# Linear attention in a one-core decoder layer: heads alternated on the array, side work in other slots, two mean squares left in PSUM

## The chip, the cores and the metric

The kernel runs on one core of a Trainium2 chip. The metric is the device time of one launch in microseconds. The core has a matrix engine (TensorE, PE), a vector engine (VectorE, DVE), a scalar engine (ScalarE, ACT), GpSimd (POOL) and a queue for transfers (SyncE, SP). Each engine works through its own list of instructions in order; they meet through semaphores.

## The reference

One layer of a decoder over 512 tokens of width 1024, in float32:

```
h = x + 0.5 * rms(SwiGLU_1(rms(x)))       # D_FF 2816
h = h +       rms(Mixer(rms(h)))
h = h + 0.5 * rms(SwiGLU_2(rms(h)))

Mixer:  z = u @ w_in, split into
  FoX:  8 heads of 64, causal softmax of q.k/8 + sum of log f, 128-query blocks
  GLA:  4 heads, keys 64, values 128, chunks of 64 tokens:
        attn = tril(q_in k_in^T);  kv = k_st^T v per chunk
        S_c  = decay * S_(c-1) + kv_(c-1)
        o    = attn v + q_in S_c          # within the chunk + across chunks
        o    = rms(o) * gain * silu(g_r)
  y = sigmoid(gate_fox) * (o_fox @ w_f) + sigmoid(gate_gla) * (o_gla @ w_g);  y @ w_out
```

## The kernel before

Precision. The large products are float32 products in three float32r matmuls: every weight tile is split into `w_hi` (ScalarE, `split` at L693) and `w_lo` (VectorE, L1197) and every activation likewise, and hi*hi, hi*lo, lo*hi are added in PSUM (L1862 to L1864). The products inside the linear attention are plain float32 matmuls, each of which becomes two instructions. A split needs the raw tile from memory (SP's queue, four buffers) and frees the buffer once the remainder is taken.

The start. While the first tiles come in, TensorE runs `WARM` matmuls of a constant (`earliest_units`, L2052), which wait for VectorE's memset of that constant (L1528). The first real products (L2054) wait for splits of the first tiles.

The mixer's slots. After the first projections the attention runs in 38 slots `sl`, a loop that each engine has in its own version. There are 32 softmax steps (8 heads x 4 query blocks); step `sl` begins in slot `sl` and its probabilities are transposed in slot `sl + 2`. Beside them run filler products: 13 feature products (`FILLERS`; the last four are the output gates `gr`) in blocks of three matmuls of 512 columns, three blocks in slots with `sl % 4` of 0 or 1, two blocks at 2, none at 3. From slot 16 on, `FILLED` ends one in slots 18, 22, 26, 30, 34, and the tile of unit f + 4 is split behind it.

The order within a slot:
- TensorE: scores of step `sl` (L2136 to L2138), filler blocks, the linear attention's work of `gla_slots`, transposes of step `sl - 2` (L2209), and in slots 7, 11, 15, ... the product of probabilities and values (L2219).
- ScalarE: head and gate copies (`heads_and_gates`), copies of the chunk scores (`attn_copies`, L1028), exponential (L1061), rounding of the transposed probabilities (L1073), in slots 8, 12, ... half a head pair (L1081), in 13, 21, 29, 37 the pair's rounding (L1085), for an output its square and the rounding of that (L1097, L1101), for a mean square its copy (L1104), the scaled probabilities (L1107), a split.
- VectorE: maximum (L1682), head and gate remainders, reciprocal, the state recurrence (L1701, L1704), remainder of the probabilities (L1709), pair sums (L1715, L1720), the gate product (L1738), the normed output and the remainder of its square (L1743, L1745), the remainder of a split.

Linear attention. `gla_steps` lists 18 steps: two key transposes (`kst`), and for each pair of heads scores (`attn`), chunk states (`kv`), outputs (`o`), mean squares (`ms`). They take two banks in turn (`gbank`), so a step waits until the one two before has been read. Head 2j has its keys in partitions 0 to 63, head 2j + 1 in 64 to 127. Before, the matmuls of one head come after those of the other: scores of a head are four matmuls of 64 rows (L2171), an output is four of 128 rows within chunks (L2190) and seven of 64 rows across chunks (L2194). A mean square is one 128x128 average over the square's two parts (L2199, L2200), which waits for the remainder at L1745. In slot 36 ScalarE takes the logarithm of all four mean squares at once (L1116), then the exponential (L1118).

Of the kernel before, what the change touches and what calls it, by code (L numbers as in the profile page):

```python
# [23 lines left out]
P = 128  # L24
# [21 lines left out]
WARM = 9  # L46
# [80 lines left out]
PAIRS = 2  # L127


def macaron_layer(nc, h_store, x_t, g1cols, x, w1g, w1u, w1d, g1post, gmpre, w_in, b_forget, w_alpha, b_alpha,  # L130
                  gla_g, w_bf, w_bg, w_out, gmpost, g2pre, w2g, w2u, w2d, g2post, out):
    with ExitStack() as ctx:
# [207 lines left out]
        def gain(g):  # L340
# [22 lines left out]
        def fill_free(f):  # L363

            before = f - 2 if f < 9 else f - 1
            if before < 0:
                return (v_lo, TT) if f == 0 else (gv_out, TT)
            kind, n = FILLERS[before]
            return {"q": (q_lo, 2 * n + 2), "k": (k_lo, 2 * n + 2), "gq": (gq_out, n + 1), "gk": (gk_out, n + 1),
                    "gr": (gr_ready, n + 1)}[kind]  # L370

# [306 lines left out]
        def _(act):  # L678
# [370 lines left out]
            for sl in range(SLOTS_B):  # L1049
                if sl in FILLED and sl >= LATE:  # L1050
                    heads_and_gates(FILLED[sl])
                for g in gla_slots.get(sl, ()):
                    if gla_steps[g][0] == "attn":
                        attn_copies(gla_steps[g][1], g)
# [31 lines left out]
                if sl == 9:  # L1086
                    act.wait_ge(a_dve, 5)
                    nc.scalar.activation(ga, gb, ACT.Exp, scale=-1.0 / TAU).then_inc(a_act, 1)
                for g in gla_slots.get(sl, ()):
# [5 lines left out]
                    if kind == "o":  # L1095
                        act.wait_ge(o_ready, n + 1)
                        nc.scalar.activation(msq[:, n, :], gbank(g), ACT.Square).then_inc(sq_ready, 1)  # L1097
                        act.wait_ge(sq_ready, n + 1)
                        if n:
                            act.wait_ge(gms_ready, n)  # L1100
                        nc.scalar.activation(sq_hi, msq[:, n, :], ACT.Copy).then_inc(sq_hi_out, 1)  # L1101
                    if kind == "ms":
                        act.wait_ge(gms_ready, n + 1)
                        nc.scalar.activation(msq[:, n, :], gbank(g), ACT.Copy).then_inc(ms_out, 1)  # L1104
# [4 lines left out]
                if sl in FILLED:  # L1109
                    v = U_FILL + FILLED[sl]  # L1110
                    split(v + 4)
# [79 lines left out]
        def _(dve):  # L1191
# [484 lines left out]
            for sl in range(SLOTS_B):  # L1676
# [7 lines left out]
                if sl in FILLED and sl >= LATE:  # L1684
                    heads_and_gates(FILLED[sl])
                if sl < NS:
# [23 lines left out]
                if sl >= 8 and sl % TT == 0:  # L1710
                    hh = sl // TT - 2
                    dve.wait_ge(half_out, hh + 1)
                    if hh >= 2:
                        dve.wait_ge(fox_hi, hh // 2)
                    V.tensor_tensor(pair_sum[FOX_D * (hh % 2):FOX_D * (hh % 2) + FOX_D, :], bank[0:FOX_D, B_OT, :], half_sum,  # L1715
                                    ALU.add).then_inc(pair_ready, 1)
                if sl >= 13 and (sl - 13) % 8 == 0:
                    p = (sl - 13) // 8
# [14 lines left out]
                if sl in gated_slots:  # L1733
                    n = gated_slots[sl]
                    dve.wait_ge(gr_ready, n + 1)
                    dve.wait_ge(on_ready, n + 1)
                    tile = arena[:, T_OG[n], :]
# [685 lines left out]
```

## Time and profile before

| | us |
|---|---|
| median of 3 runs | 1055.09 |
| lowest and highest | 1054.83, 1055.9 |
| the profiled execution's own time | 1056.04 |
| its span, first to last instruction | 1054.3 |

| engine | busy us | share of the span |
|---|---|---|
| TensorE | 1046.2 | 99% |
| VectorE | 816.1 | 77% |
| ScalarE | 568.0 | 54% |
| GpSimd | 44.7 | 4% |

Busy time is the union of an engine's instructions. Matmuls overlap in the array, so the difference of two starts, not a duration, is what one costs in a stream. The slots in question lie between about 459 and 540 us.

### The profile page before, as it was taken

What the parts mean: (1) busy time and instruction counts of PE and PEld (TensorE: products, weight loads), DVE (VectorE), ACT (ScalarE), POOL (GpSimd) and SP (SyncE); (2) the same over time, 40 slices, a digit from 0 to 9 for tenths busy, and PEclk for the clock granted to TensorE, in tenths of its full rate; (3) what the DMA queues carried; (4) which work ended last, traced back from release to release, by engine and by line L of the source; (5) the groups of instructions that cost most, each with busy time, mean ns of one, the idle gap of its engine ahead of it and who ended that gap; (6) DMA issues with size and microseconds to landing.
All of it is one profiled execution on the core that took longest, in us unless ns stands there. A gap on an engine that the chain in (4) does not pass through costs nothing.

```text
span 1054.3 us, 16505 instructions
## 1 busy us (share of the span) xinstructions
PE 1046.2 (99%) x6657; PEld 947.8 (90%) x6657; DVE 816.1 (77%) x971; ACT 568.0 (54%) x816; POOL 44.7 (4%) x98
## 2 busy tenths in 40 slices
PE   9999999999999999999999999999999999999997
PEld 7899999998888988888888999889899999998886
DVE  6998989989985583467689775558778878789964
ACT  6555455456654683567776344344454544566542
POOL 2000000000001310001000000021000000000001
PEclk9999999999999999999999999999999999999999
DMA  9623422451152553232120347315524224450052
GB/s 298 201 80 94 147 81 81 153 202 46 33 191 59 182 151 105 66 89 73 41 81 20 102 133 229 118 42 179 160 80 155 86 81 133 147 200 1 1 200 80
DMA packets 111835, 121.28 MB, mean 115 GB/s; under 512 B 6512, under 2 KB 92544, under 8 KB 111760
## 3 DMA queue, kind: packets, MB, share of 16 engines
q1 hardware_dynamic: 108544, 115.47, 34.3%
q10 hardware_dynamic: 2240, 2.11, 0.9%
q0 software_dynamic: 976, 2.66, 0.7%
q8 instruction: 53, 0.87, 0.3%
q14 instruction: 22, 0.18, 0.1%
HBM read 111.80 MB, written 6.29 MB: 112 GB/s over the span
## 4 chain that ended last, share of the span: by engine, by line
PE 91%; DVE 3%; ACT 2%; issue 1%; SPq 1%; DMA 1%; POOL 0%; ACTq 0%; DVEq 0%; POOLq 0%
PE bank L1961 13%; PE bank L1962 13%; PE bank L1960 13%; PE bank L1872 8%; PE bank L1862 5%; PE bank L2022 5%; PE bank L2023 5%; PE bank L2024 5%; PE bank L1864 5%; PE bank L1863 5%; PE bank L1927 1%; PE bank L1929 1%; PE bank L1928 1%; PE bank L2113 1%; PE bank L2112 1%
## 5 line engine op out<-in xcount | busy, mean ns | idle before, releaser
L1961 PE MATMUL bank<-tc,w_hi 128*128 128x256 f32 x576 | 163.3, 283 | 0.0
L1962 PE MATMUL bank<-tc,w_lo 128*128 128x256 f32 x576 | 163.3, 283 | 0.0
L1960 PE MATMUL bank<-tc,w_hi 128*128 128x256 f32 x576 | 163.2, 283 | 0.0
L1962 PE MATMUL bank<-u_hi,w_lo 128*128 128x256 f32 x504 | 142.9, 283 | 0.0
L1961 PE MATMUL bank<-u_lo,w_hi 128*128 128x256 f32 x504 | 142.8, 283 | 0.0
L1960 PE MATMUL bank<-u_hi,w_hi 128*128 128x256 f32 x504 | 142.8, 283 | 0.0
L1303 DVE TENSOR_TENSOR w_lo<-h,w_hi 128x1024 fp32r<-128x1024 f32 x72 | 87.8, 1222 | 33.6 <-ACT w_hi L765 33.6
L1962 PEld LDWEIGHTS bank<-tc,w_lo 128*128 128x128 f32 x576 | 110.8, 192 | 0.0
L1960 PEld LDWEIGHTS bank<-tc,w_hi 128*128 128x128 f32 x576 | 110.8, 192 | 0.0
L1961 PEld LDWEIGHTS bank<-tc,w_hi 128*128 128x128 f32 x576 | 110.8, 192 | 0.0
L1197 DVE TENSOR_TENSOR w_lo<-raw,w_hi 128x1024 fp32r<-128x1024 f32 x57 | 69.5, 1221 | 42.3 <-ACT w_hi L693 42.1
L765 ACT ACTIVATE w_hi<-h 128x1024 fp32r<-128x1024 f32 x72 | 75.8, 1053 | 41.1 <-PE bank L1962 26.0
L1960 PEld LDWEIGHTS bank<-u_hi,w_hi 128*128 128x128 f32 x504 | 96.9, 192 | 0.2
L1961 PEld LDWEIGHTS bank<-u_lo,w_hi 128*128 128x128 f32 x504 | 96.9, 192 | 0.2
L1962 PEld LDWEIGHTS bank<-u_hi,w_lo 128*128 128x128 f32 x504 | 96.9, 192 | 0.0
L2022 PE MATMUL bank<-w_hi,a_hi 128*128 128x512 f32 x224 | 87.3, 390 | 0.0
L2023 PE MATMUL bank<-w_lo,a_hi 128*128 128x512 f32 x224 | 87.3, 390 | 0.0
L2024 PE MATMUL bank<-w_hi,a_lo 128*128 128x512 f32 x224 | 87.3, 390 | 0.0
L1303 DVE TENSOR_TENSOR w_lo<-raw,w_hi 128x1024 fp32r<-128x1024 f32 x54 | 66.0, 1223 | 24.1 <-ACT w_hi L765 24.1
L693 ACT ACTIVATE w_hi<-raw 128x1024 fp32r<-128x1024 f32 x57 | 60.1, 1056 | 44.1 <-PE bank L1872 16.7
L809 ACT ACTIVATE scr<-bank 128x512 f32<-128x512 f32 x63 | 37.6, 598 | 81.8 <-PE bank L1962 81.8
L1862 PE MATMUL bank<-u_hi,w_hi 128*128 128x512 f32 x200 | 80.3, 401 | 0.1
(313 smaller groups left out, 2511.1 us busy)
## 6 DMA issues: line engine op xcount, KB each, us to landing
raw<-in_w_in SPq DMA_DIRECT2D x28, 512.0 KB, 3.9
raw<-in_ffn_w_down SPq DMA_DIRECT2D x20, 512.0 KB, 6.5
h<-in_ffn_w_gate SPq DMA_DIRECT2D x9, 1024.0 KB, 5.5
h<-in_ffn_w_up SPq DMA_DIRECT2D x9, 1024.0 KB, 8.7
raw<-in_ffn_w_gate SPq DMA_DIRECT2D x9, 1024.0 KB, 5.4
raw<-in_ffn_w_up SPq DMA_DIRECT2D x9, 1024.0 KB, 8.1
h<-in_w_in SPq DMA_DIRECT2D x6, 1024.0 KB, 7.0
h<-in_ffn_w_down SPq DMA_DIRECT2D x8, 512.0 KB, 6.6
```

The lines of the kernel that those rows point to most:

```text
L693: nc.scalar.activation(w_hi[:, slot(u), :], raw[:, slot(u), :], ACT.Copy).then_inc(hi_ready, 1)
L765: nc.scalar.activation(w_slot(w_hi, u), w_source(layer, q, n), ACT.Copy).then_inc(hi_ready, 1)
L1197: V.tensor_tensor(w_lo[:, slot(u), :], raw[:, slot(u), :], w_hi[:, slot(u), :].bitcast(F32), ALU.subtract).then_inc(lo_ready, 1)
L1303: V.tensor_tensor(w_slot(w_lo, u), w_source(layer, q, n), w_slot(w_hi, u).bitcast(F32), ALU.subtract).then_inc(lo_ready, 1)
L1862: mm(dst, w_hi[:, slot(u), w], rhs_hi[:, k - k0, :], start=k == k0, stop=False)
L1872: last = mm(bank[:, 2 * t + c, :], a[:, s, toks], w[:, s, c * HALF:(c + 1) * HALF], start=first and a is a_hi and w is w_hi, stop=final an ...
L1960: mm(dst, w_hi[:, slot(u), w], moving(n, 0, k, sums), start=first and k == 0, stop=False, skip_group_check=True)
L1961: mm(dst, w_hi[:, slot(u), w], moving(n, 1, k, sums), start=False, stop=False, skip_group_check=True)
L1962: last = mm(dst, w_lo[:, slot(u), w], moving(n, 0, k, sums), start=False, stop=k == KD // 2 - 1, skip_group_check=True)
L2022: mm(dst, a_hi[:, s, toks], w_hi[:, s, cols], start=start, stop=False, skip_group_check=True)
L2023: mm(dst, a_hi[:, s, toks], w_lo[:, s, cols], start=False, stop=False, skip_group_check=True)
L2024: last = mm(dst, a_lo[:, s, toks], w_hi[:, s, cols], start=False, stop=False, skip_group_check=True)
```

## The change

Five things change together.
- `gla_steps` runs each kind for both heads of a pair before the next kind, and the matmuls of the two heads are alternated one by one (`chunk_scores`, `chunk_states`, `chunk_outputs`). Their waits are joined: states wait for all four score copies, outputs for all four masks and the whole recurrence.
- New slots: `gla_slots`; squares and remainders by `norm_slots`, score copies by `copy_slots`, mean copies by `mean_slots`, gate products by `gated_slots` (and ahead of the reciprocal), the pair remainder by `fox_rest_slots`, splits 7 to 11 by `hi_slots` and `lo_slots`.
- The mean squares of heads 2 and 3 are not copied out; the logarithm reads their banks, so it becomes two instructions.
- The warming matmuls become 32 of 128 columns, from 9 of 512.
- VectorE writes their constant first.

```diff
-WARM = 9
+WARM = 32
...
-            gla_steps += [("attn", 2 * j), ("attn", 2 * j + 1), ("kv", 2 * j), ("kv", 2 * j + 1),
-                          ("o", 2 * j), ("ms", 2 * j), ("o", 2 * j + 1), ("ms", 2 * j + 1)]
+            gla_steps += [(kind, 2 * j + e) for kind in ("attn", "kv", "o", "ms") for e in range(2)]
...
-        gla_slots = {13: (0,), 15: (1,), 17: (2, 3), 18: (4, 5), 20: (6,), 22: (7, 8), 24: (9, 10), 25: (11, 12),
-                     26: (13,), 28: (14,), 30: (15, 16), 32: (17,)}
-        gated_slots = {25: 0, 29: 1, 33: 2, 37: 3}
+        gla_slots = {13: (0,), 15: (1,), 17: (2, 3), 18: (4, 5), 20: (6, 7), 21: (8,), 22: (9,),
+                     24: (10, 11), 25: (12, 13), 28: (14, 15), 29: (16,), 30: (17,)}
+        norm_slots = {20: 0, 21: 1, 28: 2, 29: 3}
+        copy_slots = {17: (0, 1), 25: (2, 3)}
+        mean_slots = {22: 0, 23: 1}
+        gated_slots = {23: 0, 27: 1, 31: 2, 35: 3}
+        fox_rest_slots = {13: 0, 23: 1, 31: 2, 37: 3}
+        hi_slots = {19: 7, 23: 8, 24: 9, 27: 10, 31: 11}
+        lo_slots = {22: 7, 24: 8, 25: 9, 30: 10, 33: 11}
...
                 if sl == NS + 4:
-                    act.wait_ge(ms_out, GLA_H)
-                    nc.scalar.activation(msq, msq, ACT.Ln, scale=4.0, bias=eps_t[:, :]).then_inc(gla_act, 1)
-                    act.wait_ge(gla_act, 1)
+                    act.wait_ge(ms_out, 2)
+                    act.wait_ge(gms_ready, GLA_H)
+                    nc.scalar.activation(msq[:, 2:4, :], bank[:, B_GLA[0]:B_GLA[0] + 2, :], ACT.Ln, scale=4.0,
+                                         bias=eps_t[:, :]).then_inc(gla_act, 1)
+                    nc.scalar.activation(msq[:, 0:2, :], msq[:, 0:2, :], ACT.Ln, scale=4.0, bias=eps_t[:, :]).then_inc(gla_act, 1)
+                    act.wait_ge(gla_act, 2)
...
+            V.memset(mean_g[:, :].bitcast(F32), 1.0 / GLA_DV).then_inc(hidden_ready, PAIRS)
             V.memset(eps_t[:, :], 4 * EPS).then_inc(merged, TILES)
             V.memset(bias_small[:, :], 0.0).then_inc(bias_set, 1)
             V.memset(c_neg[:, :].bitcast(F32), 0.0)
-            V.memset(mean_g[:, :].bitcast(F32), 1.0 / GLA_DV).then_inc(hidden_ready, PAIRS)
...
                 for _ in range(WARM):
-                    mm(bank[:, 7, :], mean_g[:, :], c_neg[:, :], start=True, stop=True)
+                    mm(bank[:, 7, 0:P], mean_g[:, :], mean_g[:, :], start=True, stop=True)
...
+            def chunk_scores(j, *banks):
+
+                if j == 0:
+                    pe.wait_ge(kst_copied, 2)
+                    pe.wait_ge(a_dve, 7)
+                    pe.wait_ge(k_lo, 2 * FOX_H // 2)
+                else:
+                    pe.wait_ge(ms_out, 2)
+                for t in range(TT):
+                    toks = slice(t * P, (t + 1) * P)
+                    for e in range(2):
+                        rows = slice(64 * e, 64 * e + 64)
+                        last = mm(banks[e][:, toks], arena[rows, T_GK + j, toks], arena[rows, T_GQ + j, toks],
+                                  start=True, stop=True)
+                        if t == TT - 1:
+                            last.then_inc(attn_ready, 1)
+
+            def chunk_states(j, *banks):
+
+                pe.wait_ge(kst_copied, 2)
+                pe.wait_ge(attn_copied, 4 * j + 4)
+                for c in range(NCH - 1):
+                    odd = c % 2
...
+            def chunk_outputs(j, *banks):
+
+                pe.wait_ge(attn_masked, 4 * j + 4)
+                pe.wait_ge(state_ready, (NCH - 1) * (j + 1))
+                for e in range(2):
+                    n = 2 * j + e
+                    for t in range(TT):
+                        mm(banks[e][:, t * P:(t + 1) * P], arena[:, T_GV + t, n * GLA_DV:(n + 1) * GLA_DV],
+                           intra[:, e, t, :], start=t == 0, stop=False, skip_group_check=True)
+                for c in range(1, NCH):
+                    cols = slice(c * CHUNK, (c + 1) * CHUNK)
+                    for e in range(2):
+                        rows = slice(64 * e, 64 * e + 64)
+                        last = mm(banks[e][:, cols], state[rows, c, :], arena[rows, T_GQ + j, cols],
+                                  start=False, stop=c == NCH - 1, skip_group_check=True)
...
             pe.wait_ge(on_ready, GLA_H)
-            pe.wait_ge(ms_out, GLA_H)
...
                 if f == 1:
                     pe.wait_ge(fox_lo, FOX_H // 2)
+                    pe.wait_ge(gla_act, 1)
```

## Rows read from the trace of the kernel before

**Rows 1.** Busy time, share of the span and instructions, from the page.

```profile
PE 1046.2 (99%) x6657; PEld 947.8 (90%) x6657; DVE 816.1 (77%) x971; ACT 568.0 (54%) x816; POOL 44.7 (4%) x98
```

**Rows 2.** Stage table: length, busy by engine (instructions), clock, DMA share, GB/s.

```profile
485.00:511.00 26.00, 25.41 (x165) 21.46 (x165) 16.90 (x39) 18.85 (x43) 1.49 (x4) 1.00 0.20 51
```

**Rows 3.** Order of time, TensorE's 64-row bursts: start, us, engine, line, operands, count.

```profile
476.94 1.71 PE L2171 MATMUL bank<-arena 64*128 64x128 f32 x16
...
481.02 1.37 PE L2181 MATMUL bank<-arena,scr 64*64 64x128 f32 x28
...
488.98 1.77 PE L2194 MATMUL bank<-arena,scr 64*128 64x64 f32 x14
...
504.10 1.16 PE L2171 MATMUL bank<-arena 64*128 64x128 f32 x8
...
509.31 1.09 PE L2181 MATMUL bank<-arena,scr 64*64 64x128 f32 x16
...
512.76 0.87 PE L2181 MATMUL bank<-arena,scr 64*64 64x128 f32 x12
```

**Rows 4.** Waits between 440 and 575 us: who for whom, total, times, longest.

```profile
PEld bank L2190 <- DVE scr L1704: 0.9, 1, 0.9
...
PEld bank L2171 <- ACT scr L1104: 0.5, 1, 0.5
```

**Rows 5.** Order of time after the third output's burst, slots 28 and 29.

```profile
520.85 0.55 PE L2209 MATMUL bank<-ident,scr 128*128 128x128 f32 x3
...
523.65 0.60 PE L2209 MATMUL bank<-ident,scr 128*128 128x128 f32 x4
...
523.96 0.68 DVE L1745 TENSOR_TENSOR a_lo<-scr,a_hi 128x512 fp32r<-128x512 f32 x1
...
525.96 0.63 ACT L1085 ACTIVATE a_hi<-scr 128x512 fp32r<-128x512 f32 x1
```

**Rows 6.** Order of time, TensorE in slot 22: scores, then behind two filler blocks.

```profile
493.84 0.42 PE L2136 MATMUL bank<-qk 128*128 128x384 f32 x1
...
495.79 0.39 PE L2199 MATMUL bank<-a_hi,mean_g 128*128 128x512 f32 x1
```

**Rows 7.** Order of time, ScalarE and VectorE, slots 25 and 26.

```profile
509.42 0.78 ACT L1028 ACTIVATE scr<-bank 64x256 f32<-64x256 f32 x2 [0.96 <-PE bank L2171]
...
514.55 2.27 DVE L1704 SCALAR_TENSOR_TENSOR scr<-scr,decay,bank 128x128 f32<-128x128 f32 x6
...
514.87 1.04 ACT L693 ACTIVATE w_hi<-raw 128x1024 fp32r<-128x1024 f32 x1
```

**Rows 8.** Order of time, the first 12 us.

```profile
0.86 0.06 DVE L1525 MEMSET eps_t<- 128x1 f32 x1 [0.86 <-PEq L2407]
...
1.49 0.17 DVE L1528 MEMSET mean_g<- 128x128 f32 x1
...
1.71 4.21 PE L2052 MATMUL bank<-c_neg,mean_g 128*128 128x512 f32 x9 [1.71 <-DVE mean_g L1528]
...
5.72 0.63 PE L2054 MATMUL bank<-u_hi,w_hi 128*128 128x512 f32 x1
5.72 0.33 PEld L2054 LDWEIGHTS bank<-u_hi,w_lo 128*128 128x128 f32 x1
...
7.00 0.42 PE L2054 MATMUL bank<-u_hi,w_lo 128*128 128x512 f32 x1
...
7.72 0.19 PEld L2054 LDWEIGHTS bank<-u_hi,w_lo 128*128 128x128 f32 x1
...
10.95 0.69 DVE L1543 TENSOR_TENSOR w_lo<-raw,w_hi 128x512 fp32r<-128x512 f32 x1 [0.57 <-ACT w_hi L899]
```

**Rows 9.** Order of time, two matmuls of 128 columns at the high clock, slot 16.

```profile
471.60 0.28 PE L2136 MATMUL bank<-qk 128*128 128x128 f32 x1
...
471.71 0.27 PE L2137 MATMUL bank<-qk,a_hi 128*128 128x128 f32 x1
```

**Rows 10.** Transfers, from the page: queue, count, KB each, us to landing.

```profile
raw<-in_w_in SPq DMA_DIRECT2D x28, 512.0 KB, 3.9
```

More of the change, by code:

```diff
@@ L1051, in _ @@
                     heads_and_gates(FILLED[sl])
[L1052 to L1054 removed]
+                for n in copy_slots.get(sl, ()):
+                    attn_copies(n, gla_steps.index(("attn", n)))
+                if sl in mean_slots:
+                    n = mean_slots[sl]
+                    act.wait_ge(gms_ready, n + 1)
+                    nc.scalar.activation(msq[:, n, :], gbank(gla_steps.index(("ms", n))), ACT.Copy).then_inc(ms_out, 1)
                 if sl < NS:
@@ L1108, in _ @@
                                          scale=rinv[:, sl:sl + 1]).then_inc(probs_ready, 1)
-                if sl in FILLED:
-                    v = U_FILL + FILLED[sl]
-                    split(v + 4)
+                if sl in FILLED and FILLED[sl] not in hi_slots.values():
+                    split(U_FILL + FILLED[sl] + 4)
+                if sl in hi_slots:
+                    split(U_FILL + hi_slots[sl] + 4)
                 if sl - 1 in FILLED and FILLERS[FILLED[sl - 1]][0] == "k":
@@ L1732, in _ @@
                     V.tensor_tensor(kin, kin, ga, ALU.mult).then_inc(a_dve, 1)
[L1733 to L1737, printed above, removed]
-                    V.tensor_tensor(tile, tile, arena[:, T_GR[n], :], ALU.mult).then_inc(og_raw, 1)
-                for g in gla_slots.get(sl, ()):
-                    kind, n = gla_steps[g]
-                    if kind == "o":
-                        dve.wait_ge(sq_ready, n + 1)
-                        V.tensor_scalar(arena[:, T_OG[n], :], gbank(g), gn[:, n:n + 1], None, ALU.mult).then_inc(on_ready, 1)
-                        dve.wait_ge(sq_hi_out, n + 1)
-                        V.tensor_tensor(sq_lo, msq[:, n, :], sq_hi.bitcast(F32), ALU.subtract).then_inc(sq_lo_out, 1)
-                if sl - 1 in FILLED:
+                if sl in norm_slots:
+                    n = norm_slots[sl]
+                    dve.wait_ge(sq_ready, n + 1)
+                    V.tensor_scalar(arena[:, T_OG[n], :], o_bank(n), gn[:, n:n + 1], None, ALU.mult).then_inc(on_ready, 1)
+                    dve.wait_ge(sq_hi_out, n + 1)
+                    V.tensor_tensor(sq_lo, msq[:, n, :], sq_hi.bitcast(F32), ALU.subtract).then_inc(sq_lo_out, 1)
+                if sl - 1 in FILLED and FILLED[sl - 1] not in lo_slots.values():
                     split(U_FILL + FILLED[sl - 1] + 4)
+                if sl in lo_slots:
+                    split(U_FILL + lo_slots[sl] + 4)
             def gate_t_lo(n):
@@ L2118, in _, with key_transposes @@
             pe.wait_ge(v_lo, TT)
-            read = {"kst": lambda n: (kst_copied, n + 1), "attn": lambda n: (attn_copied, 2 * n + 2),
-                    "kv": lambda n: (state_ready, (NCH - 1) * (n // 2 + 1)), "o": lambda n: (on_ready, n + 1),
-                    "ms": lambda n: (ms_out, n + 1)}
+            def key_transposes(g, n):
+                dst = gbank(g)
+                if n == 0:
+                    pe.wait_ge(gv_out, TT)
+                    pe.wait_ge(a_dve, 6)
+                else:
+                    pe.wait_ge(kst_copied, 1)
+                for t in (2 * n, 2 * n + 1):
+                    for j in range(2):
+                        c = (t % 2) * 2 * P + j * P
+                        last = nc.tensor.transpose(dst[:, c:c + P], arena[:, T_KST + j, t * P:(t + 1) * P], ident[:, :])
+                last.then_inc(kst_ready, 1)
@@ new lines, in chunk_states @@
+            def chunk_states(j, *banks):
[3 more added lines that the diff above has]
+                    odd = c % 2
+                    rows = slice(CHUNK * odd, CHUNK * odd + CHUNK)
+                    for e in range(2):
+                        hh = 2 * j + e
+                        last = mm(banks[odd][64 * e:64 * e + 64, (c // 2) * P:(c // 2 + 1) * P],
+                                  kst_tok[rows, c // 2, hh * GLA_DK:(hh + 1) * GLA_DK],
+                                  arena[rows, T_GV + c // 2, hh * GLA_DV:(hh + 1) * GLA_DV], start=True, stop=True)
+                    if c >= NCH - 3:
+                        last.then_inc(kv_ready, 1)
@@ L2185, in _ @@
-                    if kind == "o":
-                        pe.wait_ge(attn_masked, 2 * n + 2)
-                        pe.wait_ge(state_ready, (NCH - 1) * (n // 2 + 1))
-                        rows_k = slice(64 * (n % 2), 64 * (n % 2) + 64)
-                        for t in range(TT):
-                            mm(dst[:, t * P:(t + 1) * P], arena[:, T_GV + t, n * GLA_DV:(n + 1) * GLA_DV],
-                               intra[:, n % 2, t, :], start=t == 0, stop=False, skip_group_check=True)
-                        for c in range(1, NCH):
-                            cols = slice(c * CHUNK, (c + 1) * CHUNK)
-                            last = mm(dst[:, cols], state[rows_k, c, :], arena[rows_k, T_GQ + n // 2, cols],
-                                      start=False, stop=c == NCH - 1, skip_group_check=True)
-                        last.then_inc(o_ready, 1)
```

83 lines of the change are left out of this document (31 added, 52 removed).

## The prediction

> **What bounds the kernel now.** I read the page's busy times first: TensorE is busy 1046.2 of 1054.3 us [rows 1], so the time is the length of TensorE's own stream plus its few waits. The table by stage says whether another engine stands close behind where the change is made: from 485 to 511 us TensorE is busy 25.41 of 26.00, ScalarE 18.85, VectorE 16.90 [rows 2]. ScalarE and VectorE work there in turns (a maximum on VectorE, an exponential on ScalarE, a copy, a remainder on VectorE), so 18.85 and 16.90 of 26 leave little air once both must follow in turn. Then I went along TensorE in order of time for the linear attention's bursts [rows 3], to the waits for the one real stall [rows 4], and along all three engines through the slot that follows an output burst [rows 5]. Last, the first 12 us, because the warming matmuls change [rows 8].
>
> **Part 1, alternating heads.** The busy times of the bursts [rows 3]: scores 1.71 us for heads 0 and 1 together and 1.16 each for 2 and 3 (two such rows); states 1.37 for the first pair, 1.09 and 0.87 for the second; the inter-chunk half of an output 1.77, four times. A burst of 64-row matmuls for one head uses half the array. That two halves run side by side is seen in the first scores row: 16 instructions take 1.71 where 8 take 1.16, so part of head 1 already ran beside head 0. The first states row says the same (28 in 1.37, against 16 in 1.09). I take it that alternated bursts last as long as the longer head alone: scores 2 x 1.16, states 2 x 1.09, inter-chunk outputs 2 x 1.77. Saved: 4.03 - 2.32 = 1.71, 3.33 - 2.18 = 1.15, 7.08 - 3.54 = 3.54, together 6.4 us of TensorE. The intra-chunk matmuls use all rows and stay. Bounds: 0 if alternation buys nothing; 6.4 is the most. I take 6.4, since the overlap is in rows of the same lines.
>
> Two old waits may go. At the first output TensorE starts 0.90 after its last start, 0.67 beyond the usual 0.23, and its weights wait 0.9 for the recurrence; at head 3's scores it is 0.23 beyond, and the weights wait 0.5 for a mean copy [rows 4]. Moving splits 7 and 8 out of ScalarE's slots 15 and 18 (1.04 each) and their remainders out of VectorE's slots 16 and 19 lets the state recurrence (0.29 for the first copy, then 2.27 for six steps [rows 7]) end before TensorE asks, so I count both as gone: 0.9. Credit of the stage: 7.3 us.
>
> **Part 2, the new slots: what is late next.** Within a slot TensorE does scores, filler products, linear attention, and only then the transposes of the step two back. ScalarE does exponential, rounding of the transposed probabilities, head copies, and only then the square of the output and its rounding; VectorE's remainder ends the chain and the mean-square matmul waits for it.
> - Mean square 0 goes from slot 22 to 21, and 2 likewise into 29, one slot after the burst. The chain from the end of the burst is in the trace: burst over at 520.85, then ScalarE's copies, square and rounding, and VectorE's remainder ends at 523.96 + 0.68 = 524.64, 3.8 us later. TensorE has three transposes, scores and nine filler matmuls to do meanwhile: 520.85 to 523.65, 2.8 us [rows 5]. It waits 1.0 us, twice: 2.0.
> - Mean squares 1 and 3 come in slots 22 and 30. Their chain starts with the four transposes after the mean square before: 0.6 until they are ready, copy 0.5, the pair's rounding 0.63 [rows 5], square 0.63, rounding and remainder 0.76 + 0.68: 3.9. TensorE has those transposes (0.36) and scores with six filler matmuls (493.84 to 495.79, 1.95 [rows 6]): 2.3. It waits 1.6, twice: 3.2.
> - The states of heads 2 and 3 (slot 25) now wait for all four score copies. From the end of the first output burst (0), with the durations above and the starts 0.1 closer than durations as neighbours on an engine are: mean square 0 at 3.85, mean square 1 at 8.2. ScalarE: gate tanh and mean copy (0.6 each), exponential 22 at 8.9. VectorE: gate product (0.7), remainder of split 7 (1.22) to 11.1, maximum 23 to 11.8. ScalarE: exponential 23 at 11.8, copy, probabilities at 12.8, split 8 (1.04) at 13.45, exponential 24 at 14.4, copies at 15.1 and 15.6, probabilities, split 9 at 16.35, then four score copies (0.78 for two [rows 7]) 17.3 to 18.9. TensorE: slot 23 from 8.65, slot 24 from 10.7, scores burst 13.4 to 14.5, slot 25 from 14.8, at the states at 17.3. It waits 1.6.
> - VectorE then does the recurrence (2.6), a remainder, split 9's remainder (1.22) and the maximum. The transposes of slot 27 wait 0.3 for it, the scores of slot 28 0.8 for the exponential behind it: 1.1. Behind them in TensorE's queue stands the second output burst.
> - The last product of probabilities and values already waits for VectorE; 0.1 more.
> New waits: 2.0 + 3.2 + 1.6 + 1.1 + 0.1 = 8.0. Bounds: 0 if the chains shorten, 11 if the slot-25 wait doubles and each slot slips as much again. Stage: 8.0 - 7.3 = +0.7 us.
>
> **Part 3, mean squares left in their banks.** Two copies of about 0.6 (its other 512-column copies) leave ScalarE; the logarithm becomes two of half size, the same work. It stands behind the last values product, beside 48 filler-like gate matmuls (11 us) in which no TensorE wait shows: 0. If that cover were gone it would cost one more fixed part of an instruction, about 0.1. The new wait of gate unit 1 for the first logarithm is met long before. SP's queue: the later remainders of splits 7 to 11 free their raw buffers later, and the loads behind them start up to six slots (20 us) later. The first is gate unit 2's, freed in slot 22 and split in slot 31; such loads land in 3.9 us [rows 10]: 0. The masks on GpSimd follow the score copies and are done slots before the outputs: 0.
>
> **Part 4, the start.** The warming matmuls go from 9 of 512 columns to 32 of 128, and the constant is written first on VectorE: 0.86 in place of 1.49, so warming starts at 1.1 in place of 1.71. Today nine last to about 5.55 (the first real one starts at 5.72), 0.43 apart, and TensorE's clock rises from 1.2 to 2.4 GHz at about 7.0, where the durations drop from 0.63 to 0.42 [rows 8]. What a 128-column matmul with a weight load costs at the high clock is in the trace: starts 0.11 apart [rows 9], though its columns alone would need 0.06; the weight load sets the pace. At the low clock no row shows the pair. Below: 0.107, a quarter of 0.43. Above: 0.22, twice 0.11. The load's own duration grows from 0.19 to 0.33 [rows 8], by 0.14; a load of one column per clock would grow by 0.05, one that takes 0.11 at the high clock by 0.11. So I take 0.22, less a little. Then 27 to 29 are done when the clock rises at 7.0 and the rest take 0.11: real work starts at about 7.5 at the high clock. Before, 6 of its matmuls had gone by then: 6 x 0.23 = 1.3 us late, and TensorE never idles afterwards to give it back. The most an early start could bring is 0.1: the weights of the third stretch are ready at 10.95 + 0.69 = 11.64 [rows 8], where TensorE arrives at 11.83. Bounds: -0.1 and +2.5 (all 32 at the low clock end at 8.2, and the clock stays low for the first 1.3 us of the real work, as today: by 9.5 three products are done, where 14 were). Taken: +1.3.
>
> The Trainium skill (TensorE: Matmul & The Clock Gate, section LDWEIGHTS) gives a weight load as its columns over 1.2 GHz, whatever the contraction size. For 128 columns that is 107 ns; the trace agrees at the high clock, 0.11. If the rule held unchanged at the low clock, 32 would take 3.4 us, the start would wait for data instead, and its term would be -0.1, as in rival B below; the grown duration speaks against it.
>
> **The sum.** +0.7 + 1.3 = +2.0 on the profiled execution's own 1056.04 (span 1054.30 and 1.74 around it): 1058.0. That execution is 0.95 above the median of the runs shown, 1055.09, so on that scale 1057.1.
>
> **Rivals.**
> - A, faster: the saving arrives. The waits at the mean squares (5.2) stay, but ScalarE and VectorE, relieved early, keep up in slots 24 to 28, so the 2.7 of slots 25 to 28 vanish. Stage -2.1; with a start at -0.1 1052.9, with all waits but one chain gone as low as 1048. For it: both have over 7 us idle in 26 [rows 2]. Against: they work in turns, and two splits land where TensorE no longer gives them 2.7 us of output burst per head as cover. It decides when the copies of slot 25 are done before 17.3 us after the first burst.
> - B, the start costs nothing (load at the low clock 0.107, or the clock rises earlier): stage +0.7, 1055.7. For: a weight load could keep a pace of its own, and no row shows one that sets the pace at the low clock. Against: its duration grew by 0.14.
> - C, the clock rises later: start +2.5, 1058.3. For: no row fixes the moment of the rise to the start of work. Against: TensorE would be at work from 1.1 us without a break, earlier than now.
> - D, the alternation does not overlap: 6.4 comes back less the waits it would have filled (about 4): 1059.5. Against: the first scores row.
>
> **Chances.** Forecast (both waits and a late start) 0.38, A 0.24, B 0.20, C 0.12, D 0.06. A measurement of this kernel tells about 0.2% (2.1 us) from no change, so the lines are 1053.0 and 1057.2. The forecast lies on the upper one: half of it and most of C and D are slower (0.36); B and the other half same (0.38); A and the lucky side of B faster (0.26). Range 1050.8 to 1059.6; it leaves out the deepest form of A and the worst of C and D.
>
> **What would show it.** TensorE's inter-chunk row should read 28 instructions in about 1.8 us, twice. The first real matmul should start at about 7.5, not 5.7; if it starts at 4.9, the start step is wrong. Idle time before the mean-square matmuls should be 1.0, 1.6, 1.0, 1.6; if it is under 1 in all, the chain step is wrong and A holds. The states of slot 25 should wait for ScalarE's score copies. From the last values product on, every gap should be as before.

## The result: 0.6% slower, outside the forecast

The changed kernel takes 1061.1 us (median of 6 runs, 1060.4 to 1061.91), the kernel before 1055.18 beside it on the same chip (6 runs, 1054.56 to 1055.9): ratio 1.0056, 95% interval 1.0043 to 1.0069. Forecast was 1057.1, with 1059.6 as the upper end. The sum had the direction right (slower), though it gave a slower kernel a chance of 0.36 only; the size was wrong.

Three moments of the profiled execution divide its 5.7 us of longer span (1054.3 before, 1060.0 after): the first scores matmul of slot 0, the last values product, and the end. Starts in the kernel before: 412.34 and 538.23; after:

```profile
415.76 0.22 PE L2212 MATMUL bank<-qk 128*128 128x128 f32 x1
...
543.56 1.51 PE L2251 MATMUL bank<-pt,og 128*128 128x512 f32 x8
```

So everything up to slot 0 lost 3.42 us, slots 0 to 34 (called the stage below) went from 125.89 to 127.80 us (+1.91), and the rest from 516.1 to 516.4 (+0.4). The forecast had +1.3, +0.7 and 0.

The page's busy line, and the stage table over 26 and 27 us that answers to [rows 2] (start:end, length, then busy time and instructions of PE, PEld, DVE, ACT, POOL, then the granted clock, DMA share, GB/s):

```profile
PE 1046.1 (99%) x6680; PEld 947.8 (89%) x6680; DVE 816.5 (77%) x971; ACT 567.1 (54%) x815; POOL 44.6 (4%) x98
...
485.00:511.00 26.00, 23.36 (x159) 19.20 (x159) 18.11 (x42) 18.85 (x43) 0.00 (x0) 1.00 0.11 31
511.00:538.00 27.00, 22.76 (x163) 19.35 (x163) 17.95 (x38) 16.55 (x39) 1.64 (x4) 0.94 0.15 40
```

TensorE's total is what it was: up to slot 0 it is busy 4.1 us longer, because it starts 0.6 earlier and the longer start counts as work, and in slots 0 to 34 it is busy 4.4 less (120.90 against 125.26). In the stage it now idles 2.6 of 26 and 4.2 of 27 us, where 0.6 of 26 and none of 27 was idle before; neither ScalarE nor VectorE is full. They take turns.

The start, in order of time (start, duration, engine, line); it answers to [rows 8]:

```profile
0.89 0.17 DVE L1538 MEMSET mean_g<- 128x128 f32 x1 [0.89 <-PEq L2439]
...
1.11 7.09 PE L2067 MATMUL bank<-mean_g 128*128 128x128 f32 x32 [1.11 <-DVE mean_g L1538]
8.00 0.73 PE L2069 MATMUL bank<-u_hi,w_hi 128*128 128x512 f32 x1
8.53 0.63 PE L2069 MATMUL bank<-u_hi,w_lo 128*128 128x512 f32 x1
...
12.36 0.63 PE L2069 MATMUL bank<-u_lo,w_hi 128*128 128x512 f32 x2
12.82 0.40 PE L2069 MATMUL bank<-u_hi,w_hi 128*128 128x512 f32 x1
```

All 32 warming matmuls stand 0.21 us apart (the last ends at 8.2), and matmuls of 512 columns keep 0.43 between starts until about 12.3; before, that ended at 7.0. From then on they stand 0.23 apart. The clock column reads 1.00 through this stretch in both kernels, so here only the spacing shows the clock: 0.43 is also what the same matmuls keep at 516.31, 516.74 and 517.16 us, where the column does read 0.50. Below, "the pace breaks" means the moment at which 0.43 becomes 0.23.

The stage in order of time on TensorE, idle time before a row in brackets; it answers to [rows 3, 5]:

```profile
480.32 1.16 PE L2161 MATMUL bank<-arena 64*128 64x128 f32 x16
483.84 1.09 PE L2175 MATMUL bank<-arena,scr 64*64 64x128 f32 x28
...
489.98 2.02 PE L2188 MATMUL bank<-scr,arena 128*128 128x128 f32 x16 [0.37 <-DVE scr L1723]
491.93 1.78 PE L2194 MATMUL bank<-arena,scr 64*128 64x64 f32 x28
497.58 0.48 PE L2229 MATMUL bank<-a_hi,mean_g 128*128 128x512 f32 x1 [0.95 <-DVE a_lo L1758]
501.90 0.47 PE L2229 MATMUL bank<-a_hi,mean_g 128*128 128x512 f32 x1 [1.32 <-DVE a_lo L1758]
...
507.08 1.16 PE L2161 MATMUL bank<-arena 64*128 64x128 f32 x16
513.09 1.09 PE L2175 MATMUL bank<-arena,scr 64*64 64x128 f32 x28 [1.93 <-ACT scr L1036]
...
524.44 1.78 PE L2194 MATMUL bank<-arena,scr 64*128 64x64 f32 x28
530.09 0.47 PE L2229 MATMUL bank<-a_hi,mean_g 128*128 128x512 f32 x1 [0.99 <-DVE a_lo L1758]
534.41 0.47 PE L2229 MATMUL bank<-a_hi,mean_g 128*128 128x512 f32 x1 [1.33 <-DVE a_lo L1758]
```

Against [rows 3]: 28 matmuls of both heads last 1.78, where 14 of one head lasted 1.77. The brackets are the waits: the first (0.37) was 0.51 before, the others are new. One thing in no forecast stands behind the longest of them, in the clock column (third figure from the right; same columns as above):

```profile
512.00:514.00 2.00, 0.91 (x28) 0.88 (x28) 0.44 (x2) 1.47 (x5) 1.59 (x4) 1.00 0.33 73
514.00:516.00 2.00, 2.00 (x12) 1.89 (x9) 1.64 (x5) 0.73 (x2) 0.05 (x1) 0.52 0.63 189
516.00:518.00 2.00, 2.00 (x6) 1.54 (x7) 1.93 (x5) 0.26 (x1) 0.00 (x0) 0.62 0.00 0
```

The granted clock fell to its lower level, 1.2 GHz, from 514.1 to 517.5; the wait of 1.93 us had ended 1.0 before. It may not do so in every launch. Outside the profiled execution only the mean clock of a launch hints at it, and weakly (beside the first batch of experiments the kernel before has 0.997 or 0.998 in eight of 31 launches too): of the six launches of the changed kernel three have 0.997 or 0.998 (1061.35 to 1061.91 us, the profiled one among them) and three have 1.00 (1060.40 to 1060.85).

### The profile page after: what moved, and what is told of

It is laid out like the page before. It is cut to its first block, busy times and chain, and to the rows that moved or that the text cites. A ratio compares the mean times of both kernels' runs of the same rounds, so it can differ in the third digit from the quotient of the medians.

```text
span 1060.0 us, 16547 instructions
## 1 busy us (share of the span) xinstructions
PE 1046.1 (99%) x6680; PEld 947.8 (89%) x6680; DVE 816.5 (77%) x971; ACT 567.1 (54%) x815; POOL 44.6 (4%) x98
## 4 chain that ended last, share of the span: by engine, by line
PE 95%; DVE 2%; ACT 1%; issue 1%; POOL 0%; DVEq 0%; POOLq 0%; ACTq 0%
PE bank L1977 13%; PE bank L1976 13%; PE bank L1975 13%; PE bank L1887 9%; PE bank L1877 5%; PE bank L1879 5%; PE bank L1878 5%; PE bank L2037 5%; PE bank L2039 5%; PE bank L2038 5%; PE bank L2069 2%; PE bank L1942 1%; PE bank L1944 1%; PE bank L1943 1%; PE bank L2127 1%; PE bank L2129 1%
```

## Experiments

Twelve kernels in three batches; the kernel before ran beside each (medians 1055.63, 1055.48 and 1055.83). The ratios are to it. "Old start" is nine warming matmuls of 512 columns and the old order of the constants.

### The start and the stage, one at a time

**a_oldstart**: the change with the old start.

```
-WARM = 32
+WARM = 9
-            V.memset(mean_g[:, :].bitcast(F32), 1.0 / GLA_DV).then_inc(hidden_ready, PAIRS)   # first
+            ... (behind c_neg, as before)
-        mm(bank[:, 7, 0:P], mean_g[:, :], mean_g[:, :], start=True, stop=True)
+        mm(bank[:, 7, :], mean_g[:, :], c_neg[:, :], start=True, stop=True)
```

> The changed kernel with the start of before (9 warming matmuls of 512 columns, the constant written fourth). Theory S (the start costs what the two traces show, 3.4 us, and nothing downstream gives it back): 1061.1 - 3.4 = 1057.7 us, clock at 2.4 GHz from about 7.0 us. Theory M (only the mixer's slots made it slower, the start's delay was partly covered later): within 1 us of 1061.1. If the fall of the clock near 514 us hangs on where the kernel stands in time, it may go away too, and the time is 1056.5 or less.

Measured 1057.57 us, ratio 1.0016 (1.0006 to 1.0025): theory S. The clock still falls in the stage.

**b_newstart**: the kernel before with the new start alone.

> The kernel of before with only the new start (32 warming matmuls of 128 columns, the constant first). Theory S: 1055.2 + 3.4 = 1058.6 us, the clock at 2.4 GHz only near 12.3 us and the first real product at about 8.0. Theory M: within 1 us of 1055.2.

Measured 1058.44 us, ratio 1.0025 (1.0015 to 1.0034): theory S. Its trace repeats the start of the change: warming 7.09 us long, first real matmul at 8.00, and a break of pace at about 12.3:

```profile
1.11 7.09 PE L2052 MATMUL bank<-mean_g 128*128 128x128 f32 x32 [1.11 <-DVE mean_g L1525]
...
12.29 0.63 PE L2054 MATMUL bank<-u_lo,w_hi 128*128 128x512 f32 x2
12.76 0.39 PE L2054 MATMUL bank<-u_hi,w_hi 128*128 128x512 f32 x1
```

The start costs 2.8 us by the medians of b_newstart, 3.5 by those of the change and a_oldstart, which did not run side by side; the stage costs 1.9 (a_oldstart). Each alone is slower than before, so both halves of the change lose.

**b_17x128**: the kernel before with 17 warming matmuls of 128 columns, which take as long as its nine of 512 (`WARM = 17`, and the operand `mean_g` over 128 columns); the constants stay in the old order.

> The kernel of before with 17 warming matmuls of 128 columns in place of 9 of 512, the constant where it was: at 0.213 each they end at about 5.5, as the nine do, so the first real product starts when it did. It separates two parts of the start's loss. Theory L (short matmuls paced by their weight loads do not bring the clock up): the clock rises well after 7.0, near 10 to 12 us, and each microsecond of that costs half: 1056.5 to 1057.5 us. Theory T (32 were simply too long): the clock rises at 7.0 and the time is 1055.2 within 0.4.

Measured 1056.47 us, ratio 1.0006 (0.9997 to 1.0016): the time alone does not decide. The trace does:

```profile
1.71 3.89 PE L2052 MATMUL bank<-mean_g 128*128 128x128 f32 x17 [1.71 <-DVE mean_g L1528]
5.40 0.73 PE L2054 MATMUL bank<-u_hi,w_hi 128*128 128x512 f32 x1
...
9.77 0.86 PE L2054 MATMUL bank<-u_lo,w_hi 128*128 128x512 f32 x2
10.47 0.40 PE L2054 MATMUL bank<-u_hi,w_hi 128*128 128x512 f32 x1
```

The real work starts as early as ever (5.40) but runs at the low pace until about 10.5. In the eight profiled executions with the old start, the pace broke between 4.9 and 7.8. So the length of the warming alone does not explain the loss: its form counts. The late break costs less here because the real work started on time; slot 0 begins at 413.40, where it is 411.3 to 412.3 with the old start and 415.6 to 415.8 with the new one.

**b_early512**: the kernel before, the constant first, ten warming matmuls of 512 columns that read the constant's 128 columns four times.

```
+                mm(bank[:, 7, :].rearrange("p (a c) -> p a c", a=4), mean_g[:, :],
+                   mean_g[:, :].rearrange("p (o c) -> p o c", o=1).to_broadcast([P, 4, P]), start=True, stop=True)
```

> The kernel of before with the constant first and 10 warming matmuls of 512 columns (the constant read four times over), from 1.1 to about 5.55 us. If the earlier start of work brings the clock up earlier, up to 0.2 us are gained (1055.0) before the third stretch of products waits for its weights; if the clock rises at 7.0 all the same, no change.

Measured 1055.18 us, ratio 0.9994 (0.9985 to 1.0004). A gain over the kernel before is not shown. But work goes on from 1.1 us, as in the change, and on the same constant, only in long matmuls, and the pace is up with the first real one. So neither the early start of work nor the constant that is read delayed the pace in the change:

```profile
1.11 4.61 PE L2052 MATMUL bank<-mean_g 128*128 128x512 f32 x10 [1.11 <-DVE mean_g L1525]
5.54 0.41 PE L2055 MATMUL bank<-u_hi,w_hi 128*128 128x512 f32 x1
```

### Is the saving of the alternation real?

**s_headbyhead**: old start, the slots of the change, the pairs head by head.

```
-                for c in range(NCH - 1):
-                    ...
-                    for e in range(2):
+                for e in range(2):
+                    for c in range(NCH - 1):
```

(scores and outputs likewise).

> The changed kernel with the start of the kernel before (1057.57 us by itself), and the matmuls of each pair of heads issued head by head again instead of alternately; slots, waits and banks stay those of the change. Theory 1 (alternation saves what the forecast credited: two heads' 64-row matmuls run beside each other): the two output bursts grow from 3.8 us to some 5.5 each, the two score bursts from 1.16 to 1.7, the states from 1.09 to 1.37. Part of it falls into waits that are there anyway (the second score burst into the 2 us wait of slot 25), so +3.5 to +5: 1061.0 to 1062.6. Rival (it is the new places of the work, not the order of the matmuls, that changed the bursts; alternation is worth nothing): 1057.6 within 0.5.

Measured 1062.97 us, ratio 1.0069 (1.0054 to 1.0084): 5.4 over a_oldstart, theory 1 and 0.4 more than its upper end. Its bursts, and the waits among them:

```profile
476.89 1.71 PE L2161 MATMUL bank<-arena 64*128 64x128 f32 x16
480.97 1.58 PE L2175 MATMUL bank<-arena,scr 64*64 64x128 f32 x28
488.06 1.77 PE L2193 MATMUL bank<-arena,scr 64*128 64x64 f32 x14
490.85 1.77 PE L2193 MATMUL bank<-arena,scr 64*128 64x64 f32 x14
...
512.28 1.55 PE L2175 MATMUL bank<-arena,scr 64*64 64x128 f32 x28 [1.72 <-ACT scr L1036]
```

The bursts sum to 13.63 us against 8.06 alternated: 5.57 saved. Only 0.5 of it goes back into longer waits (the brackets of the stage sum to 7.21 here, 7.75 in s_meancopies below, which has the same clock in the stage), and 5.57 less 0.54 leaves 5.03, and slots 0 to 34 are 5.04 longer (132.54 against 127.50). The alternation saves its time; the new slots cost more than that.

### The new waits

**s_earlysq**: old start; square, rounding, norm and remainder right behind the exponential and the reciprocal of their slot.

```
+                if sl in norm_slots:          # ScalarE, moved up, ahead of the copy to pt
+                    ...ACT.Square...
+                    ...sq_hi...
                 if 2 <= sl < NS + 2:
                     ...pt_hi...
-                if sl in norm_slots:
```

(the same on VectorE).

> The changed kernel with the start of before, and in the four norm slots the square, its rounding, the norm and the rest are put right behind the slot's exponential and reciprocal, ahead of the copies of the transposed probabilities. Theory 1 (the waits of the mean-square matmuls, 1.1, 1.5, 1.15 and 1.5 us, come from ScalarE doing two to three copies first): each wait shrinks to 0.3 or less, 4 to 5 us go, of which 0 to 1.5 come back as waits for the delayed copies (transposes or values products): 1053 to 1055. Rival (the waits are hidden time: ScalarE or VectorE bounds these slots, so the time moves to the next wait): 1057.6 within 0.7.

Measured 1054.12 us, ratio 0.9987 (0.9977 to 0.9996): 3.45 less than a_oldstart. Waits of TensorE in the stage (who for whom, total, times, longest), where a_oldstart has 4.6 in 4 for the same remainder:

```profile
PE bank L2175 <- ACT scr L1036: 2.1, 1, 2.1
PE bank L2229 <- DVE a_lo L1730: 1.3, 2, 0.6
```

Two of the four waits are gone and the others halved (0.6 each, where 0.3 or less was expected): 3.3 of 4.6 us, and the time follows one for one. The order of the work within the slot set them; it was changed on ScalarE and VectorE together, so their shares are not known. The clock falls here too, behind the wait of 2.1.

**s_split9**: old start; split of filler 9's slot one slot later.

```
-        hi_slots = {19: 7, 23: 8, 24: 9, 27: 10, 31: 11}
-        lo_slots = {22: 7, 24: 8, 25: 9, 30: 10, 33: 11}
+        hi_slots = {19: 7, 23: 8, 25: 9, 27: 10, 31: 11}
+        lo_slots = {22: 7, 24: 8, 26: 9, 30: 10, 33: 11}
```

> The changed kernel with the start of before, and the split of filler 9's slot moved one slot later on ScalarE (from 24 to 25) and on VectorE (from 25 to 26), so that the copies of the second chunk scores start about 1 us earlier. Theory 1 (the wait of the second chunk states is set by this split, and the fall of the granted clock behind it by the length of the wait): the gap of 2.3 us before the states becomes 1.2 to 1.4, the clock stays high in the stage, 1.0 us of wait and 1 to 1.5 us of slow matmuls go: 1055.1 to 1055.6. Rival 1 (the clock falls whatever this wait is): only the 1.0 us goes, 1056.6. Rival 2 (the split comes back as a wait one slot later): 1057.6.

Measured 1055.45 us, ratio 1.0000 (0.9990 to 1.0010): 2.1 less than a_oldstart, the size that theory 1 gave. The wait for the score copies is halved and the clock stays up (waits as above; the table's last figures are clock, DMA share, GB/s):

```profile
PE bank L2175 <- ACT scr L1036: 1.0, 1, 1.0
...
512.00:514.00 2.00, 1.81 (x14) 1.75 (x14) 1.85 (x6) 1.40 (x4) 0.00 (x0) 1.00 0.03 8
514.00:516.00 2.00, 2.00 (x11) 1.65 (x11) 2.00 (x3) 0.59 (x2) 0.00 (x0) 1.00 0.03 5
```

The size was right for half a wrong reason, as the next two runs show.

### What the fall of the clock costs

**s_fill**: old start; seven matmuls of 512 columns whose result nobody reads ahead of the second states.

```
+                if j:
+                    pe.wait_ge(pair_ready, 5)
+                    for _ in range(7):
+                        mm(bank[:, B_OT, :], mean_g[:, :], c_neg[:, :], start=True, stop=True)
                 pe.wait_ge(kst_copied, 2)
```

> The changed kernel with the start of before, and seven matmuls of 512 columns whose result nobody reads (into the bank of the values product, free at this moment) stand ahead of the second chunk states, where TensorE otherwise waits 2.1 us for the copies of the scores. Theory 1 (the granted clock falls because TensorE waits that long): with 1.6 us of the wait filled, the clock stays at 2.4 GHz, the states start at the same time as before, and the 1.1 us of slow matmuls behind them go: 1056.2 to 1056.8 against 1057.57. Rival (the clock falls there for another reason, such as what ran in the microseconds before, or the matmuls in the wait only add work): the fall stays and the time is 1057.6 or more.

Measured 1057.27 us, ratio 1.0015 (1.0006 to 1.0025). The clock stayed at 1.00 from 480 to 518 us, and yet only 0.3 us went, within the spread of a_oldstart's runs (1056.75 to 1058.09), and 0.1 if each is taken against the kernel before beside it. Neither answer holds in full: the slow matmuls went, and two waits took their place:

```profile
506.76 1.79 PE L2171 MATMUL bank<-c_neg,mean_g 128*128 128x512 f32 x7
...
513.34 0.41 PE L2245 MATMUL bank<-ident,scr 128*128 128x128 f32 x2 [0.31 <-DVE pt L1728]
515.55 0.33 PE L2216 MATMUL bank<-qk 128*128 128x128 f32 x1 [0.58 <-ACT scr L1072]
```

**s_meancopies**: old start; the mean squares of heads 2 and 3 copied out of their banks again.

```
-        mean_slots = {22: 0, 23: 1}
+        mean_slots = {22: 0, 23: 1, 30: 2, 31: 3}
...
-                    nc.scalar.activation(msq[:, 2:4, :], bank[:, B_GLA[0]:B_GLA[0] + 2, :], ACT.Ln, scale=4.0,
+                    nc.scalar.activation(msq, msq, ACT.Ln, scale=4.0, bias=eps_t[:, :]).then_inc(gla_act, 2)
```

> The changed kernel with the start of before, and the mean squares of heads 2 and 3 are copied out of their banks again by ScalarE, at the head of slots 30 and 31, with one logarithm over all four heads at the end. Theory 1 (forecast, Part 3: leaving them in the banks is worth nothing, the copies fit ScalarE's idle time): 1057.6 within 0.5. Rival (each copy of 0.6 us stands ahead of an exponential that TensorE's chain waits for): +0.6 to +1.2, 1058.2 to 1058.8.

Measured 1057.75 us, ratio 1.0018 (1.0009 to 1.0028): theory 1; leaving them in the banks is worth nothing that can be measured. The profile gave more than was asked. Up to slot 29 this kernel is a_oldstart, and its wait before the states is the same 1.94 us, but in this execution the clock did not fall:

```profile
508.67 1.09 PE L2172 MATMUL bank<-arena,scr 64*64 64x128 f32 x28 [1.94 <-ACT scr L1036]
513.14 0.41 PE L2238 MATMUL bank<-ident,scr 128*128 128x128 f32 x2 [0.31 <-DVE pt L1725]
515.35 0.33 PE L2209 MATMUL bank<-qk 128*128 128x128 f32 x1 [0.58 <-ACT scr L1072]
```

against this of a_oldstart, from the stage table:

```profile
510.00:512.00 2.00, 2.00 (x9) 1.90 (x9) 1.82 (x6) 0.99 (x2) 0.00 (x0) 0.55 0.42 126
512.00:514.00 2.00, 2.00 (x7) 1.51 (x7) 1.97 (x4) 0.07 (x1) 0.00 (x0) 0.60 0.00 0
```

From slot 0 to the last values product a_oldstart takes 127.78, s_meancopies 127.50, s_fill 127.52. So the fall costs 0.3 us net between these executions: while TensorE runs slowly, VectorE and ScalarE catch up, and the waits of 0.31 and 0.58 behind it vanish. The launches do not speak against it: the two of a_oldstart with a mean clock of 0.997 took 1057.46 and 1057.67, in the middle of the eight others (0.999 or 1.00), and three of s_meancopies' ten have 0.997 as well (1057.40 to 1057.58, within the others' 1056.97 to 1058.12). In the changed kernel, however, the launches with the lower mean are 0.5 to 1.5 us longer than the others. No trace was taken of one without the fall, so whether it costs more there, or the moment at which the pace breaks differs too, stays open.

The s_split9 gain of 2.0 in the stage (125.81) is then 0.9 of shorter wait, 0.6 of the scores wait behind it, which is gone, 0.3 of clock, and 0.1 to 0.2 unassigned. I put the 0.6 down to VectorE, which no longer has the remainder of split 9 (1.22 us) ahead of slot 26's maximum; that half was not moved alone.

### Putting it together

**s_both**: the two edits together, old start.

> Both edits together, the early squares and the later split of filler 9. Theory 1 (the two waits are independent, both are on the path of TensorE): the savings add, 1050.5 to 1053. Rival (ScalarE bounds the stage once the waits are short, so they do not add): no better than the better one of the two by more than 0.5.

Measured 1052.23 us, ratio 0.9969 (0.9958 to 0.9981). Savings of 3.45 and 2.1 give 5.3 together: they nearly add, theory 1. Slots 0 to 34 take 122.19.

**f_both_early512**: the same with the start of b_early512.

> Early squares, later split of filler 9, and a start with the constant set first and ten warming matmuls of 512 columns that read the constant itself, its 128 columns four times. Theory 1 (stage and start are independent; this start gained 0.3 to 0.45 on the kernel before): 1051.5 to 1052.2 against 1052.23 of the same stage with the old start. Rival (the start's effect is only the moment at which the clock rises, which varies by itself): 1052.2 within 0.5, and the rise stands in the trace at no other time than in the kernel before.

Measured 1051.70 us, ratio 0.9961 (0.9946 to 0.9976), the fastest of all: 4.1 us under the kernel before beside it by medians, and 9.4 under the changed kernel, which did not run beside it. The 0.5 against s_both is what theory 1 gave, but the two profiles differ in the same sense as those of one start do (pace breaks at 7.8 and at about 6.4), so the start's share is not proven.

**f_best**: the same with the transposes ahead of mean squares and states in slots 21, 25 and 29 (`side_work` is TensorE's loop over `gla_slots`).

```
+                if sl not in (21, 25, 29):
+                    side_work()
                 if 2 <= sl < NS + 2:
                     ...transposes...
+                if sl in (21, 25, 29):
+                    side_work()
```

> The same, and in slots 21, 25 and 29 TensorE does the transposes of the probabilities ahead of the mean-square matmuls or the chunk states. Theory 1 (the waits of 0.8, 1.3 and 0.8 us that remain there are partly filled by transposes of 0.35 to 0.45 us each, whose inputs are there already): 0.8 to 1.2 less than the kernel without this, 1050.5 to 1051.3. Rival (the transposes wait for the scaled probabilities of the slot before, which ScalarE does just ahead, so that only the order of two waits changes): no difference over 0.3.

Measured 1051.92 us, ratio 0.9963 (0.9949 to 0.9977): the rival's time, though not by the wait that it named. Where f_both_early512 waits 1.2 for the score copies and 0.3 for the remainder of the probabilities, it reads:

```profile
PE bank L2176 <- ACT scr L1036: 0.7, 1, 0.7
PE bank L2246 <- DVE pt L1734: 0.7, 1, 0.7
```

The transposes fill 0.5 us of the first wait and the second grows by 0.4. The states start when the copies are done, as before; on VectorE the recurrence (2.6 us) follows them, and the remainder of the probabilities, for which TensorE waits, follows the recurrence.

## Why the prediction was wrong, step by step

- **What bounds the kernel**: right. TensorE's stream and its waits make the time: s_earlysq took 3.3 us from its waits and 3.45 us from the time.
- **Part 1, bursts**: right to 0.02 us. Scores 1.16 twice, states 1.09 twice, inter-chunk outputs 1.78 twice: 8.06 where [rows 3] sum to 14.44, 6.4 saved. The Trainium skill (TensorE: Matmul & The Clock Gate, section The mechanism) says that small matmuls overlap when they sit in different row groups of the array; 28 in 1.78 us against 14 in 1.77 agrees.
- **Part 1, the old waits**: mostly wrong, by 0.6. The wait before head 3's scores is gone, but of the 0.23 credited for it 0.1 is the distance that every score burst keeps (0.32 or 0.33, at 476.94 before and 480.32 after). The one before the first output is not gone: 0.37 idle, 0.53 beyond the usual distance of 0.23, still for the recurrence. The relieved VectorE does reach the recurrence earlier, 1.37 us by the rows below (each against its slot 0), but TensorE, with its shorter bursts, asks 1.22 earlier too; the step counted the first and not the second.

```profile
485.51 2.26 DVE L1704 SCALAR_TENSOR_TENSOR scr<-scr,decay,bank 128x128 f32<-128x128 f32 x6
...
487.56 2.26 DVE L1723 SCALAR_TENSOR_TENSOR scr<-scr,decay,bank 128x128 f32<-128x128 f32 x6
```

- **Part 2, mean squares**: right. Forecast 1.0, 1.6, 1.0, 1.6; measured beyond the distance of 0.23 between starts 1.1, 1.5, 1.15, 1.5: 5.2 both ways. The durations of the second chain add up to 3.8 and not 3.9, which would have given the 1.5 measured.
- **Part 2, states of heads 2 and 3**: forecast 1.6, measured 2.1 beyond the same distance. ScalarE's copies began 17.65 us after the end of the first output burst (at 511.36), not 17.3.
- **Part 2, slots 27 and 28**: forecast 0.3 and 0.8; where the clock stays up they are 0.3 and 0.6 (s_meancopies). In the changed kernel's own profile 3.4 us of slow matmuls cover them. The fall of the clock is a mechanism the forecast did not have; its net price is 0.3 by the profiles of the kernels with the old start. The 0.1 at the last values product did not come: it starts 0.41 after its predecessor in both kernels.
- Stage together: +1.9 for +0.7. The difference of 1.2 is 0.6 (old waits), 0.5 (states) and 0.3 (clock), less 0.2 in slots 27 and 28 and 0.1 at the last values product, which leaves 0.1 unassigned. The 0.4 behind the last values product is mostly a wait of 0.2 of the gate matmuls for VectorE's last filler result (L1665).
- **Part 3**: right, 0 (s_meancopies, within 0.2).
- **Part 4, the start: the step that failed**, with 2.1 of the 3.7 us that the sum was short. Its price of a 128-column pair at the low clock (taken "0.22, less a little") measured 0.213 (15 more of them, 32 against 17, last 3.20 us longer), and by 7.0 us about 27 were done, in "27 to 29". What failed is "are done when the clock rises at 7.0": the moment was read off the kernel before and held fixed while the work ahead of it was exchanged. It came at 12.3. The bounds of the step had the mechanism, as rival C ("no row fixes the moment of the rise"), but allowed 1.3 us of slow real work; it was 4.3. The argument against C, that TensorE is at work from 1.1 us without a break, was the error: b_newstart and b_17x128 are without a break too and speed up at 12.3 and 10.5, while b_early512, at work from 1.1 us in long matmuls, does so at 5.5. Why short matmuls and long ones differ in this, no run shows.
- The moment of the rise varies between executions of the old start: with it at 4.9 to 5.7 slot 0 starts at 411.3 to 411.6, with it at 7.0 to 7.8 at 412.3. The profile of before was one of the late ones; against an early one the new start costs 4.3. That the medians of the single parts (2.8 and 1.9) sum to 4.7 and not 5.9 is inside their intervals.

The Trainium skill (TensorE: Matmul & The Clock Gate, section LDWEIGHTS) gives a weight load as its columns over 1.2 GHz. That is 0.107 us for 128. The pairs of load and matmul stand 0.11 apart at 2.4 GHz, which agrees, but 0.213 at 1.2 GHz, twice as far, so the rule alone gives the distance at one of the two levels only, and the measurement decides. Whether the load got slower there (its own duration goes from 0.19 to 0.33) or load and matmul follow one another, no run separates. The forecast had set the rule aside because of the grown duration, and the 0.213 bears that choice out.

## What to carry to other kernels

A moment at which the chip changes its state, read off one kernel, belongs to the work ahead of it: exchange that work, and the moment is an unknown with a range of its own. Warm TensorE with long matmuls, not with many short ones: here the 32 short ones cost 2.8 to 3.5 us. When the work of two heads is merged into one burst, what follows either of them starts at the end of both; put what feeds the next burst (here square and rounding) at the head of the slot, and keep long side work off the engine whose copies are waited for. These two moves of a few lines turned slots 0 to 34 from 1.9 us longer than before into 3.7 us shorter (122.19 in s_both against 125.89).

## What the runs showed of the hardware

- Pairs of a weight load and a matmul of 128 columns stand 0.11 us apart at 2.4 GHz and 0.213 at 1.2 GHz, at either level twice the quarter of what a matmul of 512 columns takes (0.23 and 0.43). A short matmul with a load of its own thus costs double its columns.
- In these kernels short matmuls back to back did not bring the clock up as long ones did. Low pace until 12.3 us after 32 of 128 columns from 1.1 us on (twice), until 10.5 after 17 from 1.7 us on; with nine or ten of 512 columns until 4.9 to 7.8, in eleven executions.
- A wait of 1.9 to 2.1 us between small waits was followed by a fall of the granted clock in three of four profiles (the change, a_oldstart and s_earlysq, not s_meancopies); with waits of 1.72 us or less in that place it fell in none of six. The mean clocks of the launches (0.997 in two of ten of a_oldstart, 0.997 or 0.998 in three of six of the change and eight of ten of s_earlysq) hint, weakly, that it also differs between launches of one kernel. What decides it stays open.
- A slow stretch of TensorE can cost less than its length when it would wait for the other engines next: 3.4 us at half clock cost 0.3 between a_oldstart and the two kernels like it whose clock stayed up.
